# Prompt attention scores from a 64-row and a 128-row product in place of three 128-row products

## The chip, the cores and the metric

The kernel runs on one core of a Trainium2 chip. The metric is the device time of one execution in microseconds; a kernel's time is the median of its runs.

## The reference, cut to what matters

The reference is one inference step of a hybrid decoder layer: a prompt of 1024 tokens and a decode batch of 8 x 8 tokens go through a projection, dilated window attention (8 heads of 64), retention, an output projection and an MLP. The change touches the attention of the prompt alone. There, for each head, three branches (window, dilation) of the same queries, keys and values are combined by their softmax denominators:

```python
def _dilated_branch_prompt(q, k, v, window, dil):
    ...
    s = jnp.einsum('brcqhd,brckhd->brchqk', qb, kw).astype(F32) * (HEAD_DIM ** -0.5)
    ...
    valid = (dist[None] >= 0) & (dist[None] <= n) & (kg >= 0)
    p, lse = _masked_softmax(s, valid[None, None, :, None])
    o = jnp.einsum('brchqk,brckhd->brcqhd', p, vw.astype(F32))
```

## The kernel before, in words

The kernel runs its stages one after the other: modulation, projection, prompt attention, sample heads, sample (cache) attention, prompt retention, output projection, MLP. Each stage is a block with one instruction stream per engine, ordered by semaphores, and a barrier of all engines stands between stages (line 177 for those that clear their semaphores). The change lies in stage_prompt_attention, from line 692.

The stage computes the three branches at once: a score gets a bias, the logarithm of the number of branches in which its key is valid, or -1e30. Heads are handled in four pairs, as a loop of two rounds (i) with two pairs (s = 0, 1) written out in each. A pair's queries and keys lie as token tiles of 128 tokens x 128 columns, two heads of 64 side by side. PE transposes them (turn_heads, line 788, 8 transposes for queries into PSUM banks 0 and 1, 8 for keys into banks 2 and 3), so that rows 0 to 63 hold head 0 and rows 64 to 127 head 1.

Scores are made in the type fp32r from a high and a low part of each operand: high is the value rounded to fp32r, low is what is left. ScalarE takes the high parts out of PSUM (take_queries, line 829, which also scales and is done once for each head, 64 rows by 1024 columns; take_keys, line 835, all 128 rows at once). VectorE takes the low parts (low_parts, line 888: two passes of 64 rows for queries, one pass of 128 rows for keys, k_lo, line 896). Queries are held in tiles of 128 rows per head, whose other 64 rows are zero, so that a product over 128 rows with the keys of both heads gives the scores of one; the zeros are written once, by four memsets of VectorE at the stage's start (line 862), and ScalarE waits for them before it does anything (line 819).

A pair has 16 units (head, query tile of 128 rows). Head 0 goes through query tiles 0 to 7, head 1 through 7 to 0 (line 719). A unit with tile q has (q + 1) x 128 keys, in chunks of up to 512 keys, one PSUM bank each: tiles 0 to 3 have one chunk, tiles 4 to 7 two. For each chunk PE makes three products into the same bank (lines 770 and 771):

```python
for a, (x, y) in enumerate(((q_hi, k_hi), (q_hi, k_lo), (q_lo, k_hi))):
    mm = pe.matmul(out, x[h][:, q * P:(q + 1) * P], y[:, c:e], start=(a == 0), stop=(a == 2))
```

A unit then goes on: VectorE adds the bias and takes the row maximum (score, line 869, the instruction of line 874), ScalarE takes the exponential with its sum (line 827), VectorE divides (normalise, line 881), PE transposes the probabilities into banks 4 and 5 (turn, line 774), ScalarE copies them out (probT, line 849), PE multiplies with the values (values, line 780, products of 128 rows by 64 columns of weights into banks 6 and 7).

The order of PE's stream is written by hand: scores run three units ahead (scores(u + 3), turn(u + 1), values(u) in the loop from line 803). For s = 0 the transposes of the next pair's queries and keys stand near the end of the loop (line 806). ScalarE takes the next pair's queries after the probT copy of unit 14 and its keys after that of unit 15 (lines 850 to 853), and then copies the finished output of the pair out of PSUM (mix_hi, line 855). VectorE makes the next pair's low parts after its last normalise (line 905), then mix_lo, which waits for mix_hi (line 907), and then the first score of the next pair. Before the second round of the loop the order is another: mix_hi and mix_lo first, then the transposes, queries, keys and low parts. PE starts a pair's scores when all of its low parts are there (line 798). SP loads pairs ahead and GpSimd rotates their queries and keys; for pairs 2 and 3 SP waits for heads_free (line 733), which PE raises at a pair's end.

Of the kernel before, what the change touches and what calls it, by code (L numbers as in the profile page):

```python
# [20 lines left out]
F32 = mybir.dt.float32  # L21
F32R = mybir.dt.float32r
ALU = mybir.AluOpType
# [3 lines left out]
P = 128  # L27
D = 1024
KT = D // P
S = 1024  # L30
TT = S // P
# [4 lines left out]
H, HD = 8, 64  # L36
# [650 lines left out]
def banks(ps, first, n):  # L687

    return ps[:, first:first + n, :].rearrange("p b c -> p (b c)")


def stage_prompt_attention(nc, io, ps, ident, mix_hi, mix_lo, heads, smp):
# [6 lines left out]
    with st.ctx:  # L699
# [4 lines left out]
        q_hi = [st.sb(f"qhi{h}", [P, S], F32R) for h in range(2)]  # L704
        q_lo = [st.sb(f"qlo{h}", [P, S], F32R) for h in range(2)]
        k_hi, k_lo = st.sb("khi", [P, S], F32R), st.sb("klo", [P, S], F32R)
# [4 lines left out]
        zeroed, heads_free, turned, hi_done, split_done = (st.sem(n) for n in (  # L711
            "zeroed", "heads_free", "turned", "hi_done", "split_done"))
# [42 lines left out]
        def _(pe):  # L755
            pe.sem_inc(prob_turned, 3)
            pe.sem_inc(pv_done, 2)
            with pe.Fori(0, 2) as i:
                for s in range(2):
                    base = i * 2 * UNITS + s * UNITS  # L760

                    def scores(u):
                        h, q = unit(u)
                        if u >= 2:
                            pe.wait_ge(scored, base + u - 1)
                        width = (q + 1) * P
                        for c in range(0, width, CH):
                            e = min(width, c + CH)
                            out = banks(ps, 2 * (u % 2), 2)[:, c:e]
                            for a, (x, y) in enumerate(((q_hi, k_hi), (q_hi, k_lo), (q_lo, k_hi))):  # L770
                                mm = pe.matmul(out, x[h][:, q * P:(q + 1) * P], y[:, c:e], start=(a == 0), stop=(a == 2))
                        mm.then_inc(made, 1)
# [25 lines left out]
                    pe.wait_ge(split_done, 3 * (2 * i + s) + 3)  # L798
# [19 lines left out]
        def _(act):  # L818
            act.wait_ge(zeroed, 4)
            with act.Fori(0, 2) as i:  # L820
                for s in range(2):
# [7 lines left out]
                    def take_queries(s):  # L829
                        act.wait_ge(turned, 2 * (2 * i + s) + 1)  # L830
                        for h in range(2):
                            rows = slice(HD * h, HD * (h + 1))
                            act.mul(q_hi[h][rows, :], banks(ps, 0, 2)[rows, :], SCALE).then_inc(hi_done, 1)

                    def take_keys(s):
                        act.wait_ge(turned, 2 * (2 * i + s) + 2)
                        act.copy(k_hi[:], banks(ps, 2, 2)).then_inc(hi_done, 1)
# [20 lines left out]
        def _(dve):  # L858
            for x in (q_hi, q_lo):
                for h in range(2):  # L860
                    rows = slice(HD * (1 - h), HD * (2 - h))
                    dve.memset(x[h][rows, :].bitcast(F32), 0.0).then_inc(zeroed, 1)
            dve.wait_ge(zeroed, 4)
            dve.wait_ge(bias_in, 16)
            with dve.Fori(0, 2) as i:
                for s in range(2):
# [21 lines left out]
                    def low_parts(s):  # L888
                        for h in range(2):
                            rows = slice(HD * h, HD * (h + 1))  # L890
                            dve.wait_ge(hi_done, 3 * (2 * i + s) + h + 1)
                            dve.scalar_tensor_tensor(out=q_lo[h][rows, :], in0=banks(ps, 0, 2)[rows, :], scalar=SCALE,
                                                     in1=q_hi[h][rows, :].bitcast(F32), op0=ALU.mult,
                                                     op1=ALU.subtract).then_inc(split_done, 1)
                        dve.wait_ge(hi_done, 3 * (2 * i + s) + 3)
                        dve.tensor_tensor(k_lo[:], banks(ps, 2, 2), k_hi[:].bitcast(F32), ALU.subtract).then_inc(split_done, 1)
# [1850 lines left out]
```

## Time and profile before

| | |
|---|---|
| Median of 3 runs | 1938.46 us (1932.27 to 1939.40) |
| The profiled execution's own time | 1934.55 us |
| Its span, first to last instruction | 1932.6 us |
| Mean granted TensorE clock | 0.935 |
| Busy PE, weight loads, VectorE, ScalarE, GpSimd | 1699.1, 1371.6, 837.4, 550.3, 563.3 us |
| Prompt attention stage in the profile | about 421 to 631 us |

PE is TensorE's matmul side and PEld its weight loads, which can run under matmuls. The ends of matmuls are modelled in the profile, so the distance from one start to the next tells more than the length of one. The granted clock is 1.00 where TensorE ran at 2.4 GHz and 0.50 where it ran at 1.2 GHz.

### The profile page before, as it was taken

The page shows a single profiled execution, that of the slowest core. Times are in us where ns is not written, and L with a number is a line of the kernel's source. Part 1 is how long each engine was busy: PE and PEld are TensorE (multiplying, and loading weights), DVE is VectorE, ACT ScalarE, POOL GpSimd, SP SyncE. Part 2 cuts the span into 40 slices and gives each one's busy share as a digit, 9 for nine tenths or more (in the row PEclk, how much of TensorE's full clock was granted, in tenths as well). Part 3 has the DMA queues.
Part 4 walks back from the last instruction along what each step waited for, and adds up shares of the span by engine and source line. Part 5 has one row for each costly group of instructions (what it writes and reads, how often), then busy time and mean ns, then how long its engine had stood idle before and what let it go on. Part 6 is the DMA issues. An engine that isn't in the chain of part 4 may idle for free. (4 is left out here: it accounts for less than half of the span.)

```text
span 1932.6 us, 22382 instructions
## 1 busy us (share of the span) xinstructions
PE 1699.1 (88%) x8256; PEld 1371.6 (71%) x8256; DVE 837.4 (43%) x1556; ACT 550.3 (28%) x814; POOL 563.3 (29%) x272
## 2 busy tenths in 40 slices
PE   6599999979999478876699689999999999999983
PEld 1488888867777366655578568787878787878862
DVE  3921222026555345565556323333333333333489
ACT  0322222225555145552334321111111111111121
POOL 0332323335000015586000242222222222222354
PEclk9699999989999689996799899999999999999997
DMA  7534443362210667783052211111111111111122
GB/s 271 191 125 162 165 158 117 125 182 57 67 33 0 152 187 218 219 252 118 7 186 87 77 44 44 44 43 43 43 43 43 43 43 43 43 43 43 44 87 93
DMA packets 136813, 192.69 MB, mean 100 GB/s; under 512 B 10155, under 2 KB 84955, under 8 KB 136612
## 3 DMA queue, kind: packets, MB, share of 16 engines
q1 hardware_dynamic: 124630, 169.42, 27.8%
q10 hardware_dynamic: 12128, 22.55, 3.1%
q8 instruction: 32, 0.52, 0.1%
q14 instruction: 23, 0.19, 0.0%
HBM read 162.94 MB, written 29.00 MB: 99 GB/s over the span
## 5 line engine op out<-in xcount | busy, mean ns | idle before, releaser
L2286 POOL TENSOR_TENSOR mlp_w_lo<-w_room,mlp_w_hi 128x2048 fp32r<-128x2048 f32 x31 | 143.6, 4634 | 320.7 <-ACT mlp_w_hi L2282 320.6
L2587 PE MATMUL ps<-mix_hi,mlp_w_hi 128*128 128x512 f32 x512 | 204.7, 400 | 15.2 <-DVE mlp_w_lo L2286 9.7
L2485 DVE TENSOR_TENSOR x<-x,ps 128x512 f32<-128x512 f32 x224 | 153.9, 687 | 142.4 <-PE ps L2658 141.4
L2464 DVE TENSOR_TENSOR mlp_h_lo<-mlp_pos,mlp_h_hi 128x512 fp32r<-128x512 f32 x64 | 69.3, 1083 | 332.9 <-ACT mlp_h_hi L2388 330.8
L2587 PE MATMUL ps<-mix_lo,mlp_w_hi 128*128 128x512 f32 x512 | 204.6, 400 | 0.0
L2587 PE MATMUL ps<-mix_hi,mlp_w_lo 128*128 128x512 f32 x512 | 203.3, 397 | 0.0
L2658 PE MATMUL ps<-mlp_w_hi,mlp_h_hi 128*128 128x512 f32 x448 | 175.9, 393 | 5.5 <-DVE mlp_h_lo L2464 4.0
L2658 PE MATMUL ps<-mlp_w_hi,mlp_h_lo 128*128 128x512 f32 x448 | 174.4, 389 | 0.0
L2658 PE MATMUL ps<-mlp_w_lo,mlp_h_hi 128*128 128x512 f32 x448 | 174.4, 389 | 0.0
L603 POOL TENSOR_TENSOR inp_a_lo<-inp_room,inp_a_hi 128x2048 fp32r<-128x2048 f32 x24 | 110.5, 4604 | 216.3 <-ACT inp_a_hi L649 216.3
L628 PE MATMUL ps<-inp_whi,z_hi 128*128 128x512 f32 x384 | 151.5, 395 | 10.6 <-DVE inp_wlo L575 7.8
L628 PE MATMUL ps<-inp_wlo,z_hi 128*128 128x512 f32 x384 | 150.6, 392 | 0.0
L628 PE MATMUL ps<-inp_whi,z_lo 128*128 128x512 f32 x384 | 150.4, 392 | 0.0
L1828 POOL TENSOR_TENSOR cache_v_lo<-cache_V,cache_v_hi 128x2048 fp32r<-128x2048 f32 (+1 forms) x19 | 74.1, 3902 | 227.4 <-ACT cache_v_hi L1770 227.4
L2338 POOL TENSOR_TENSOR mlp_pos<-mlp_pos 128x512 f32<-128x512 f32 x64 | 66.6, 1040 | 215.5 <-ACT mlp_pos L2394 215.5
L2587 PEld LDWEIGHTS ps<-mix_hi,mlp_w_hi 128*128 128x128 f32 x512 | 97.1, 190 | 41.0 <-DVE mlp_w_lo L2286 10.1
L2394 ACT ACTIVATE mlp_pos<-ps 128x512 f32<-128x512 f32 x64 | 38.3, 598 | 295.9 <-PE ps L2587 295.9
L583 DVE TENSOR_TENSOR x_s<-ps,x_s 9x256 f32<-9x256 f32 x24 | 9.9, 412 | 242.3 <-ACT x_s L666 242.3
L2587 PEld LDWEIGHTS ps<-mix_hi,mlp_w_lo 128*128 128x128 f32 x512 | 97.0, 189 | 23.0
L2587 PEld LDWEIGHTS ps<-mix_lo,mlp_w_hi 128*128 128x128 f32 x512 | 97.1, 190 | 22.7
L2658 PEld LDWEIGHTS ps<-mlp_w_hi,mlp_h_hi 128*128 128x128 f32 x448 | 84.1, 188 | 25.3 <-issue 8.3
L2409 ACT CAST mlp_hs<-ps 128x128 fp32r<-128x128 f32 x16 | 4.2, 266 | 332.3 <-PE ps L2602 332.3
(365 smaller groups left out, 3506.1 us busy)
## 6 DMA issues: line engine op xcount, KB each, us to landing
w_room<-in_w_ff SPq DMA_DIRECT2D x32, 1024.0 KB, 6.8
inp_room<-in_w_ada SPq DMA_DIRECT2D x16, 1024.0 KB
proj<-inp_row ACTq DMA_DIRECT2D x54, 256.0 KB, 2.3
x<-in_cache_k SPq DMA_DIRECT2D x48, 256.0 KB, 5.3
cache_V<-in_cache_v SPq DMA_DIRECT2D x48, 256.0 KB, 4.7
mod_w<-in_w_ada SPq DMA_DIRECT2D x4, 2048.0 KB, 15.2
x<-in_x_prompt SPq DMA_DIRECT2D x16, 512.0 KB, 9.5
inp_room<-in_w_ada_f SPq DMA_DIRECT2D x8, 1024.0 KB
```

Of the source, the lines that this page charges most:

```text
L583: dve.tensor_tensor(a_row[j % 2], ps[0:NC, 6 + j % 2, 0:AW_CH], a_row[j % 2], ALU.add).then_inc(added, 1)
L603: pool.tensor_tensor(a_lo[:], a_raw[s], a_hi[:].bitcast(F32), ALU.subtract).then_inc(a_ready, 1)
L628: mm = pe.matmul(bank, z[:, k, cols], w[s][:, k, :], start=(k == 0 and a == 0), stop=(k == KT - 1 and a == len(parts) - 1))
L1828: eng.tensor_tensor(v_part(1, q, c), V[:, first:first + count, :], v_part(0, q, c).bitcast(F32), ALU.subtract).then_inc(v_ready, 1)
L2286: pool.tensor_tensor(lo, raw, hi.bitcast(F32), ALU.subtract).then_inc(ready, 1)
L2338: pool.tensor_tensor(x, x, x, ALU.mult).then_inc(sq_done, 1)
L2394: act.activation(pos[u % 2][:], ps[:, u, :], ACT.Relu).then_inc(relu_done, 1)
L2409: act.copy(hs[s][:, :, 0:NS], turned_s(ps)).then_inc(hs_hi, 1)
L2464: dve.tensor_tensor(h_lo[s][:, j, cols], pos[u % 2][:], h_hi[s][:, j, cols].bitcast(F32), ALU.subtract).then_inc(h_ready, 1)
L2485: dve.tensor_tensor(dst, dst, ps[:, 5 + o % 3, :], ALU.add).then_inc(added, 1)
L2587: mm = pe.matmul(ps[:, u, :], w[:, k, j * P:(j + 1) * P], z[:, k, rows], start=(k == 0 and a == 0), stop=(k == KT - 1 and a == 2))
L2658: mm = pe.matmul(out, h, w, start=(a == 0), stop=(a == len(parts) - 1))
```

## The change

The two mixed products, high queries with low keys and low queries with high keys, become one product over 128 rows. For it each head has a tile of queries (q_both) with the low part in its own 64 rows and the high part in the other head's rows, and a tile of keys (k_both) with the high part in its own rows and the low part in the other rows. The high parts are multiplied in a product over the head's own 64 rows. q_hi becomes one tile for both heads.

ScalarE takes the queries in one pass of 128 rows, the keys in two passes of 64 rows (one per head), and then copies the high queries of each head to the other partition half (two passes of 64 rows from SBUF to SBUF, semaphore moved). VectorE makes the low queries in two passes as before, both waiting for the one pass of ScalarE, and the low keys in two passes of 64 rows, which read one partition half and write the other. The four memsets and their wait are gone. PE waits for split_done (four passes) and for the first move before a pair's scores, and for the second move before unit 8.

```diff
--- before.py
+++ after.py
@@ -701,15 +701,17 @@
         bias_in, roped = heads.bias_in, heads.roped
         tmp = [st.sb(f"tmp{s}", [P, 2 * TT, 2, HALF]) for s in range(4)]
 
-        q_hi = [st.sb(f"qhi{h}", [P, S], F32R) for h in range(2)]
-        q_lo = [st.sb(f"qlo{h}", [P, S], F32R) for h in range(2)]
-        k_hi, k_lo = st.sb("khi", [P, S], F32R), st.sb("klo", [P, S], F32R)
+        q_hi = st.sb("qhi", [P, S], F32R)
+        q_both = [st.sb(f"qboth{h}", [P, S], F32R) for h in range(2)]
+        k_both = [st.sb(f"kboth{h}", [P, S], F32R) for h in range(2)]
+        OWN = [slice(HD * h, HD * (h + 1)) for h in range(2)]
+        OTHER = OWN[::-1]
         prob = [st.sb(f"prob{s}", [P, S]) for s in range(3)]
         probT = [st.sb(f"probT{s}", [P, S]) for s in range(2)]
         top, neg, total, inv = (st.sb(n, [P, UNITS]) for n in ("top", "neg", "total", "inv"))
         waited = st.sb("waited", [P, 1])
-        zeroed, heads_free, turned, hi_done, split_done = (st.sem(n) for n in (
-            "zeroed", "heads_free", "turned", "hi_done", "split_done"))
+        heads_free, turned, hi_done, split_done, moved = (st.sem(n) for n in (
+            "heads_free", "turned", "hi_done", "split_done", "moved"))
         made, scored, neg_done, exp_done, inv_done, prob_done, prob_turned, probT_done, pv_done, mix_hi_done = (
             st.sem(n) for n in ("made", "scored", "neg_done", "exp_done", "inv_done", "prob_done",
                                 "prob_turned", "probT_done", "pv_done", "mix_hi_done"))
@@ -763,12 +765,15 @@
                         h, q = unit(u)
                         if u >= 2:
                             pe.wait_ge(scored, base + u - 1)
+                        if u == TT:
+                            pe.wait_ge(moved, 2 * (2 * i + s) + 2)
                         width = (q + 1) * P
                         for c in range(0, width, CH):
                             e = min(width, c + CH)
                             out = banks(ps, 2 * (u % 2), 2)[:, c:e]
-                            for a, (x, y) in enumerate(((q_hi, k_hi), (q_hi, k_lo), (q_lo, k_hi))):
-                                mm = pe.matmul(out, x[h][:, q * P:(q + 1) * P], y[:, c:e], start=(a == 0), stop=(a == 2))
+                            at = slice(q * P, (q + 1) * P)
+                            pe.matmul(out, q_hi[OWN[h], at], k_both[h][OWN[h], c:e], start=True, stop=False)
+                            mm = pe.matmul(out, q_both[h][:, at], k_both[h][:, c:e], start=False, stop=True)
                         mm.then_inc(made, 1)
 
                     def turn(u):
@@ -795,7 +800,8 @@
                     if s == 0:
                         turn_heads(0, 0)
                         turn_heads(0, 1)
-                    pe.wait_ge(split_done, 3 * (2 * i + s) + 3)
+                    pe.wait_ge(split_done, 4 * (2 * i + s) + 4)
+                    pe.wait_ge(moved, 2 * (2 * i + s) + 1)
                     scores(0)
                     scores(1)
                     scores(2)
@@ -816,7 +822,6 @@
 
         @block.scalar
         def _(act):
-            act.wait_ge(zeroed, 4)
             with act.Fori(0, 2) as i:
                 for s in range(2):
                     base = i * 2 * UNITS + s * UNITS
@@ -828,13 +833,15 @@
 
                     def take_queries(s):
                         act.wait_ge(turned, 2 * (2 * i + s) + 1)
-                        for h in range(2):
-                            rows = slice(HD * h, HD * (h + 1))
-                            act.mul(q_hi[h][rows, :], banks(ps, 0, 2)[rows, :], SCALE).then_inc(hi_done, 1)
+                        act.mul(q_hi[:], banks(ps, 0, 2), SCALE).then_inc(hi_done, 1)
 
                     def take_keys(s):
                         act.wait_ge(turned, 2 * (2 * i + s) + 2)
-                        act.copy(k_hi[:], banks(ps, 2, 2)).then_inc(hi_done, 1)
+                        for h in range(2):
+                            act.copy(k_both[h][OWN[h], :], banks(ps, 2, 2)[OWN[h], :]).then_inc(hi_done, 1)
+                        act.wait_ge(hi_done, 3 * (2 * i + s) + 1)
+                        for h in range(2):
+                            act.copy(q_both[h][OTHER[h], :], q_hi[OWN[h], :].bitcast(F32)).then_inc(moved, 1)
 
                     if s == 0:
                         take_queries(0)
@@ -856,11 +863,6 @@
 
         @block.vector
         def _(dve):
-            for x in (q_hi, q_lo):
-                for h in range(2):
-                    rows = slice(HD * (1 - h), HD * (2 - h))
-                    dve.memset(x[h][rows, :].bitcast(F32), 0.0).then_inc(zeroed, 1)
-            dve.wait_ge(zeroed, 4)
             dve.wait_ge(bias_in, 16)
             with dve.Fori(0, 2) as i:
                 for s in range(2):
@@ -886,14 +888,15 @@
                                           ALU.mult).then_inc(prob_done, 1)
 
                     def low_parts(s):
+                        dve.wait_ge(hi_done, 3 * (2 * i + s) + 1)
                         for h in range(2):
-                            rows = slice(HD * h, HD * (h + 1))
-                            dve.wait_ge(hi_done, 3 * (2 * i + s) + h + 1)
-                            dve.scalar_tensor_tensor(out=q_lo[h][rows, :], in0=banks(ps, 0, 2)[rows, :], scalar=SCALE,
-                                                     in1=q_hi[h][rows, :].bitcast(F32), op0=ALU.mult,
+                            dve.scalar_tensor_tensor(out=q_both[h][OWN[h], :], in0=banks(ps, 0, 2)[OWN[h], :], scalar=SCALE,
+                                                     in1=q_hi[OWN[h], :].bitcast(F32), op0=ALU.mult,
                                                      op1=ALU.subtract).then_inc(split_done, 1)
-                        dve.wait_ge(hi_done, 3 * (2 * i + s) + 3)
-                        dve.tensor_tensor(k_lo[:], banks(ps, 2, 2), k_hi[:].bitcast(F32), ALU.subtract).then_inc(split_done, 1)
+                        for h in range(2):
+                            dve.wait_ge(hi_done, 3 * (2 * i + s) + h + 2)
+                            dve.tensor_tensor(k_both[h][OTHER[h], :], banks(ps, 2, 2)[OWN[h], :], k_both[h][OWN[h], :].bitcast(F32),
+                                              ALU.subtract).then_inc(split_done, 1)
 
                     if s == 0:
                         low_parts(0)
```

## Rows read from the trace of the kernel before

**Rows 1.** Stretch: length, busy PE, PEld, DVE, ACT, POOL; clock, DMA, GB/s.

```profile
488.00:526.00 38.00, 38.00 (x266) 31.75 (x265) 20.50 (x75) 20.05 (x40) 3.80 (x5) 1.00 0.10 29
```

**Rows 2.** Waits of 421 to 631 us: us in total, times, longest.

```profile
PE ps L771 <- DVE att_klo L896: 15.8, 4, 7.2
```

**Rows 3.** Timeline, PE, score products (start, length in us), one unit each.

```profile
449.95 0.50 PE L771 MATMUL ps<-att_khi,att_qhi 128*128 128x512 f32 x1
450.29 0.39 PE L771 MATMUL ps<-att_klo,att_qhi 128*128 128x512 f32 x1
450.52 0.40 PE L771 MATMUL ps<-att_khi,att_qlo 128*128 128x512 f32 x1
...
458.65 0.28 PE L771 MATMUL ps<-att_klo,att_qhi 128*128 128x256 f32 x1
458.77 0.28 PE L771 MATMUL ps<-att_khi,att_qlo 128*128 128x256 f32 x1
...
473.96 0.28 PE L771 MATMUL ps<-att_klo,att_qhi 128*128 128x128 f32 x1
474.07 0.28 PE L771 MATMUL ps<-att_khi,att_qlo 128*128 128x128 f32 x1
```

**Rows 4.** Timeline, PE, retention stage, 64-row and 128-row products.

```profile
922.91 0.49 PE L1280 MATMUL ps<-ret_state,ret_qdT 64*128 64x128 f32 x2
923.33 0.49 PE L1278 MATMUL ps<-x,ret_sT 128*128 128x128 f32 x2
...
928.13 1.84 PE L1265 MATMUL ps<-ret_qT,ret_kT 64*128 64x128 f32 x15
```

**Rows 5.** Timeline, PE, sample attention, 8-row products behind 128-row ones.

```profile
736.71 0.40 PE L1664 MATMUL ps<-cache_v_lo,cache_probT 128*128 128x512 f32 x1
737.04 0.49 PE L1668 MATMUL ps<-cache_vn_hi,cache_probT 8*128 8x512 f32 x1
737.38 0.39 PE L1668 MATMUL ps<-cache_vn_lo,cache_probT 8*128 8x512 f32 x1
```

**Rows 6.** Timeline, start of the stage.

```profile
421.08 3.67 PE L792 MATMUL ps<-ident,x 128*128 128x128 f32 x16 [3.76 <-PEq L486]
...
425.77 1.28 ACT L833 ACT_TABLE_LOAD   x1 [7.83 <-DVE att_qlo L862]
...
431.90 0.47 PE L771 MATMUL ps<-att_khi,att_qhi 128*128 128x128 f32 x1 [7.15 <-DVE att_klo L896]
```

**Rows 7.** Timeline, end of pair 0 and start of pair 1.

```profile
478.32 2.48 DVE L892 SCALAR_TENSOR_TENSOR att_qlo<-ps,att_qhi 64x1024 fp32r<-64x1024 f32 x2 [2.19 <-ACT att_qhi L833]
...
479.35 0.27 ACT L849 COPY att_probT<-ps 128x128 f32<-128x128 f32 x1
...
480.42 1.03 ACT L855 CAST mix_hi<-ps 128x1024 f32 x1
...
481.96 1.21 DVE L908 TENSOR_TENSOR mix_lo<-ps,mix_hi 128x1024 f32 x1
...
482.10 0.33 PE L771 MATMUL ps<-att_khi,att_qhi 128*128 128x128 f32 x1 [2.00 <-DVE att_klo L896]
...
483.10 0.28 DVE L874 CUSTOM_DVE_ANT_0 att_prob<-ps,x 128x128 f32<-128x128 f32 x1
```

**Rows 8.** Groups by line and shape, ScalarE, a copy from SBUF to SBUF.

```profile
L2073 ACT CAST outp_whi<-w_room 128x1024 fp32r<-128x1024 f32 x8 | 8.1, 1046 | 9.8 <-DMA w_room<-in_w_out 8.2 <-PEq L1031 1.6
```

**Rows 9.** Timeline, first score product of pair 2.

```profile
534.02 0.47 PE L771 MATMUL ps<-att_khi,att_qhi 128*128 128x128 f32 x1 [4.63 <-DVE att_klo L896]
```

**Rows 10.** The stretches' view again: two boundaries, then retention.

```profile
476.90:488.00 11.10, 8.01 (x40) 5.54 (x40) 8.64 (x26) 7.30 (x15) 0.74 (x2) 0.85 0.47 142
577.60:590.40 12.80, 10.30 (x47) 7.26 (x46) 8.63 (x26) 7.65 (x16) 0.00 (x0) 0.73 0.00 0
...
901.00:916.70 15.70, 10.48 (x30) 7.41 (x30) 7.13 (x4) 1.71 (x2) 3.18 (x1) 0.50 0.22 71
...
921.50:928.10 6.60, 6.60 (x38) 4.86 (x38) 3.95 (x9) 2.26 (x7) 0.00 (x0) 1.00 0.04 11
```

## The prediction

> **What bounds the kernel now.** I read the page first (TensorE is busy 88% of the span), then the stretches of the one stage that the diff touches, then its waits, then single instructions. The attention stage lasts from 421 to 631 us, four head pairs of 16 units each. In the steady part of a pair TensorE has no gap at all: 38.00 us busy of 38.00 in pair 1, while VectorE has 20 and ScalarE 20 [rows 1]. So there a TensorE instruction more or less moves the end one for one. Between pairs it is not TensorE: it stands still 15.8 us in four waits, all for the low part of the keys on VectorE [rows 2]. Two prices decide, then: what a product costs on TensorE, and what the split of queries and keys costs on ScalarE and VectorE between pairs. The stage ends at a barrier of all engines and nothing after it is under way before, so I take its change to the end of the kernel one for one.
>
> **Products removed.** Today a unit makes three products per chunk of up to 512 keys; there are 96 chunks (48 of 512 keys, 16 each of 384, 256 and 128). From start to start a product of 512 takes 0.23 us, of 256 0.12, of 128 0.11 [rows 3]; 384 I put between, 0.175. One product per chunk goes: 48 x 0.23 + 16 x (0.175 + 0.12 + 0.11) = 17.5 us. That the remaining one has 64 rows saves nothing: products of 64 rows ran at 0.112 us each for 128 columns (15 in 1.84 us, the last one's 0.27 us tail taken off) [rows 4], as the 128-row ones did [rows 3].
>
> **Switches added.** The new pair alternates 64 rows and 128 rows. The retention stage does the same today: a 128-row product, then a 64-row product into the same accumulation, with no wait between. Each product there is two instructions, which at 0.112 would take 0.22 us; they take 0.42 [rows 4], so 0.20 us goes at each change of row count. The other place is an 8-row product behind 128-row ones, 512 columns, the same type as the scores: 0.33 us up to it and 0.34 behind its start, 0.67 where 0.46 is the steady pace [rows 5], so 0.21 for one change. Both sit close, in both directions; I take 0.20. A unit's scores are entered from the 64-column value products, a change that exists already (the first product starts 0.34 before the second, where 0.23 is the pace [rows 3]). So a unit with one chunk gains one switch; a unit with two chunks gains three. A pair has 8 of each, so 8 + 24 = 32 switches, 128 in all: 25.6 us. TensorE's net work is 25.6 - 17.5 = +8.1 us. Of that the first three units of a pair lie under VectorE's latency (they have one chunk, 128 to 384 keys: 3 x 0.20 - 0.405 = 0.2 us per pair, 0.8 in all): **+7.3 us**. Bounds: without a cost of switching -17.5, with 0.22 each 28.2 - 17.5 = +10.7. The page "TensorEngine Tiling (Array Packing)" of the Trainium skill, Key Properties, says that changing the tiling mode drains the engine, which speaks against this change, and gives no price; the trace agrees with 0.20 us.
>
> **Start of the stage.** Four memsets and the wait on them go. Today the queries are taken only behind them: the table load starts at 425.77, scores at 431.90 [rows 6]. Without them the load (1.28 us) runs under the transposes that began at 421.08 at half clock, half of whose 3.67 us make the queries ready near 423.1. One ScalarE pass (1.03 us for 1024 columns [rows 7]; VectorE's take 1.24 with 64 rows and 1.21 with 128, so the rows don't count [rows 7]) and then VectorE's four passes of 1.24 (two for queries, now two for keys where there was one): 423.1 + 1.03 + 4 x 1.24 = 429.1. ScalarE's two key passes and two moves end about then and hold up nothing. **-2.8 us**. Bounds: -4 (if the transposes are taken earlier) and -1.2 (no overlap of the table load).
>
> **Between pairs 0 and 1, 2 and 3.** Here ScalarE's order matters. Today: queries, last probT copy (479.35), keys, mix_hi (480.42), and VectorE: low parts, mix_lo at 481.96, first score at 483.10 [rows 7]. The new order has one query pass, so the copy waits only for its transpose (about 479.0), then two key passes, two moves, and only then mix_hi. A move is a ScalarE copy from SBUF to SBUF into the other partition half; no such copy to other partitions stands in the trace, and the nearest is a copy of 1024 columns within its partitions, 1.05 us [rows 8]. I take 1.05, with nothing and twice as much as bounds, for lack of a nearer row. So 479.15 + 2 x 1.02 + 2 x 1.05 = 483.2, mix_hi until 484.2, and **behind mix_hi waits mix_lo on VectorE, and behind mix_lo the first score**, which comes at 484.3 + 1.14 = 485.4 instead of 483.1: +2.3 us each, **+4.5 us** for two. TensorE's own start of scores moves only 1.2 us (VectorE's fourth pass), which the late score covers. If moves cost nothing, the boundary is set by that fourth pass and costs 1.2 each, 2.4 in all; if twice as much, 8.7.
>
> **Between pairs 1 and 2.** Queries and keys are taken after mix_lo here, so only VectorE's extra pass counts, scores start 1.2 us behind 534.02 [rows 9]; moves end before. **+1.2 us**.
>
> **Clock.** TensorE stands still longer at the two boundaries. The stretch around the first had granted clock 0.85, around the second 0.73 [rows 10]. A pair's first units then run at the lower pace; what part of that VectorE's latency hides I can't read, so I add **+1.0 us** for a longer time at 1.2 GHz (0 to 3).
>
> GpSimd has no instruction in the diff; SP's loads of the next pair wait on heads_free, two pairs ahead of use, so both queues only shift.
>
> **Sum**: +7.3 - 2.8 + 4.5 + 1.2 + 1.0 = +11.2 us. The profiled execution took 1934.55 us, so 1945.8 against it. The median of the runs is 1938.46, 3.9 above that execution; carried onto it, the changed kernel comes at **1949.7 us**. Half a per cent (9.7 us) is about what a measurement of this kernel tells from no change; the sum sits just beyond it.
>
> **Rivals.**
> *The switch is free for these products* (chance 0.07). TensorE does 17.5 us less, of which 1.6 in the first three units is hidden: -15.9, with the +3.9 of start, boundaries and clock: -12.0, **1926.5 us**. For it: the loads of 128-row weights hide entirely at the pace of [rows 3]. Against it stand [rows 4, 5]. The page "TensorE: Matmul & The Clock Gate" of the Trainium skill, Part 2, has a rule that would do this: weight loads are pulled ahead of running matmuls if they go to the background buffer; by that rule 1926.5 us, but [rows 4] don't show it.
> *Half a switch* (0.08): only the drain or only the exposed load, 0.10 us. 12.8 - 17.5 + 3.9 = -0.8, **1937.7 us**, no change to see.
> *The clock falls* (0.13). The engine streams for a smaller part of each unit. In the retention stage the same alternation ran at granted clock 0.50 for all of 906 to 917, and at 1.00 in 922 to 928 [rows 10], so it neither raises the clock by itself nor drops it at once. If each pair spends some 7 us more at half clock at its start, TensorE would lose 3.5 us if it alone set the time, and as VectorE sets a good part of these units, some 2; that is +8 on the sum: **1958 us**. It decides once a pair's start stays at 1.2 GHz for ten us.
> *The boundaries cost nothing*, because the late score is absorbed by later slack or the moves run under something (0.05): 7.3 - 2.8 + 1.2 = +5.7, **1944 us**.
> The forecast has 0.67: its own range, from the bounds of moves, start, clock and a switch of 0.17 to 0.22 us, is +6 to +15. About two thirds of that lies over 9.7.
>
> **Chances.** Slower by over 0.5%: 0.44 of the forecast plus the clock, 0.57. Within 0.5%: 0.23 of the forecast, half a switch and idle boundaries, 0.36. Faster: 0.07. The range must reach from just above half a switch to the clock case, 1940 to 1959; it leaves out the free switch, most of the half switch and the tails.
>
> **What would show it.** The 64-row and 128-row score products should start about 0.43 us apart at 512 columns; 0.23 makes the free switch right. PE busy should still fill the steady stretch. ScalarE should show four passes of 1.0 between the last probT copy and mix_hi, and the first score of pairs 1 and 3 should come about 1.2 us after mix_hi ends. The first score product should start near 429. Were TensorE idle in the steady part, or the clock under 0.9 there, the sum would be wrong in kind.

## The result and the profile after

The changed kernel takes 1968.88 us (median of 4 runs, 1961.43 to 1971.02) against 1938.13 us before: 1.6% slower, ratio 1.0159, 95% interval 1.0134 to 1.0185, or +30.8 us. The forecast said slower, by 11.2 us, and the time lies outside its range. The profiled execution is the fastest of the four, 1961.43 us. In it the attention stage ends 35.5 us later than before (its last mix_hi starts at 663.85 instead of 628.36), and some 8 us of that come back in later stages; the other three executions are 7 to 10 us slower as a whole, so the median need not hold that.

The page, its first lines and the row of the granted clock:

```profile
span 1959.8 us, 22209 instructions
...
PE 1729.4 (88%) x8160; PEld 1370.8 (70%) x8160; DVE 836.4 (43%) x1556; ACT 558.7 (29%) x822; POOL 563.6 (29%) x272
...
PEclk9799999978877878997879899999999999999997
```

There are 96 instructions fewer on PE and 30 us more of PE busy. The clock row is the first clue: in slices 9 to 14, where most of the attention stage lies, it reads 7 or 8, where before it reads 9, and 8 once.

The view by stretch shows why. Its columns are as in [rows 1]: length, busy PE, PEld, DVE, ACT and POOL, granted clock, DMA. The stretches are all those of the changed kernel's attention stage at granted clock 0.50, and one at 1.00 (the third) between them:

```profile
419.60:450.30 30.70, 24.73 (x73) 15.82 (x73) 16.04 (x44) 14.14 (x25) 11.18 (x10) 0.50 0.75 195
487.80:508.30 20.50, 19.62 (x53) 11.67 (x54) 11.06 (x41) 7.76 (x19) 4.23 (x6) 0.50 0.31 92
508.30:541.00 32.70, 32.70 (x213) 24.62 (x211) 15.09 (x56) 15.81 (x31) 0.00 (x0) 1.00 0.01 2
545.90:569.80 23.90, 20.11 (x55) 12.20 (x55) 12.73 (x43) 10.27 (x22) 4.17 (x6) 0.50 0.21 64
607.30:634.60 27.30, 26.32 (x73) 16.20 (x74) 12.75 (x48) 10.58 (x23) 0.00 (x0) 0.50 0.00 0
```

And the same view of the kernel before, again all stretches of the stage at 0.50:

```profile
419.70:436.80 17.10, 8.43 (x32) 6.66 (x32) 10.38 (x25) 6.32 (x11) 3.64 (x6) 0.50 0.98 247
484.60:488.00 3.40, 3.26 (x9) 2.14 (x10) 2.56 (x13) 2.12 (x7) 0.74 (x2) 0.50 0.58 173
532.40:539.20 6.80, 4.74 (x15) 3.35 (x15) 5.03 (x20) 1.97 (x7) 4.19 (x6) 0.50 0.11 32
583.60:590.40 6.80, 6.50 (x20) 4.32 (x20) 4.16 (x23) 3.25 (x10) 0.00 (x0) 0.50 0.00 0
```

102.4 us at 1.2 GHz after, 34.1 us before. Every pair now has 20 to 30 us at half clock at its start, and there TensorE hardly stands still once its products run (19.62 us busy of 20.50 in pair 1). Once a pair is at 2.4 GHz it stays there to its end, although the alternation goes on.

The timeline of PE gives the two prices of a switch, which is a change between 64 and 128 rows from one product to the next. At 2.4 GHz, answering to [rows 3]:

```profile
453.42 0.50 PE L775 MATMUL ps<-att_kboth,att_qhi 64*128 64x512 f32 x1
453.85 0.50 PE L776 MATMUL ps<-att_kboth,att_qboth 128*128 128x512 f32 x1
454.28 0.49 PE L775 MATMUL ps<-att_kboth,att_qhi 64*128 64x512 f32 x1
454.70 0.50 PE L776 MATMUL ps<-att_kboth,att_qboth 128*128 128x512 f32 x1
```

and at 1.2 GHz:

```profile
498.52 0.79 PE L775 MATMUL ps<-att_kboth,att_qhi 64*128 64x512 f32 x1
499.25 0.80 PE L776 MATMUL ps<-att_kboth,att_qboth 128*128 128x512 f32 x1
499.97 0.58 PE L775 MATMUL ps<-att_kboth,att_qhi 64*128 64x256 f32 x1
```

0.43 us from start to start at full clock is 0.20 more than the 0.23 of [rows 3]. At half clock it is 0.72 to 0.73, where two products of 128 rows stood 0.43 us apart in the kernel before:

```profile
586.19 0.63 PE L771 MATMUL ps<-att_klo,att_qhi 128*128 128x512 f32 x1
586.62 0.63 PE L771 MATMUL ps<-att_khi,att_qlo 128*128 128x512 f32 x1
```

The weight loads show what changes. Behind a switch a load starts together with its own product (453.85 and 454.28 above):

```profile
453.85 0.19 PEld L776 LDWEIGHTS ps<-att_kboth,att_qboth 128*128 128x128 f32 x1 [0.25 <-issue]
454.28 0.18 PEld L775 LDWEIGHTS ps<-att_kboth,att_qhi 64*128 64x128 f32 x1 [0.24 <-issue]
```

In the kernel before, the load for the product at 450.52 [rows 3] starts 0.22 us ahead of it, under the product before:

```profile
450.30 0.19 PEld L771 LDWEIGHTS ps<-att_khi,att_qlo 128*128 128x128 f32 x1
```

Where in a pair the time goes can be read from VectorE's score passes. In pair 1, those of units 9 and 15, before and then after:

```profile
504.12 1.08 DVE L874 CUSTOM_DVE_ANT_0 att_prob<-ps,x 128x896 f32<-128x896 f32 x1 [1.37 <-issue]
523.20 0.29 DVE L874 CUSTOM_DVE_ANT_0 att_prob<-ps,x 128x128 f32<-128x128 f32 x1 [1.01 <-issue]
517.93 1.08 DVE L876 CUSTOM_DVE_ANT_0 att_prob<-ps,x 128x896 f32<-128x896 f32 x1 [1.55 <-issue]
537.52 0.29 DVE L876 CUSTOM_DVE_ANT_0 att_prob<-ps,x 128x128 f32<-128x128 f32 x1 [1.04 <-issue]
```

19.08 us before and 19.59 after, at 2.4 GHz and alike in all four pairs: half a microsecond more. From unit 0 to unit 9, where the half clock lies, the four pairs together take 86.3 us before and 116.2 after. So 30 of the stage's 35.5 us arise in the first nine units of the pairs, in the profiled executions.

Between pairs 0 and 1 the timeline of all engines, answering to [rows 7]:

```profile
483.18 0.27 ACT L856 COPY att_probT<-ps 128x128 f32<-128x128 f32 x1 [0.63 <-PE ps L782]
483.34 2.04 ACT L841 CAST att_kboth<-ps 64x1024 fp32r<-64x1024 f32 x2
...
485.28 2.11 ACT L844 CAST att_qboth<-att_qhi 64x1024 fp32r<-64x1024 f32 x2
487.42 1.01 ACT L862 CAST mix_hi<-ps 128x1024 f32 x1
487.69 0.36 PE L775 MATMUL ps<-att_kboth,att_qhi 64*128 64x128 f32 x1 [3.75 <-DVE att_kboth L898]
...
488.60 1.23 DVE L911 TENSOR_TENSOR mix_lo<-ps,mix_hi 128x1024 f32 x1 [1.04 <-ACT mix_hi L862]
...
489.75 0.29 DVE L876 CUSTOM_DVE_ANT_0 att_prob<-ps,x 128x128 f32<-128x128 f32 x1
```

Four ScalarE passes stand between the last probT copy and mix_hi, mix_lo waits for mix_hi (1.04 us idle ahead of it), and the first score for mix_lo. That score comes 6.57 us behind the last probT copy, 2.8 more than the 3.75 of [rows 7]. TensorE stands still for 3.75 us, 1.75 more than in [rows 7], until VectorE's fourth pass is done. A move to the other partition half takes 1.05 us, like a copy within the partitions [rows 8].

### The profile page after: what moved, and what is told of

It is laid out like the page before. It is cut to its first block and busy times, and to the rows that moved or that the text cites. A ratio compares the mean times of both kernels' runs of the same rounds, so it can differ in the third digit from the quotient of the medians.

```text
span 1959.8 us, 22209 instructions
## 1 busy us (share of the span) xinstructions
PE 1729.4 (88%) x8160; PEld 1370.8 (70%) x8160; DVE 836.4 (43%) x1556; ACT 558.7 (29%) x822; POOL 563.6 (29%) x272
```

## The experiments

All medians are set against the kernel before on the same chip; microseconds are the ratio less one, times 1936. "Half clock" is the time at granted clock 0.50 in the profiled execution, summed over the whole stretches that overlap the stage; the kernel before has 34. "The stage" in us is the time from its first transpose to its last mix_hi in that one execution: 207.3 before, 242.8 in the changed kernel.

| run | products and their rows | ratio (interval) | us | half clock |
|---|---|---|---|---|
| changed kernel | 64, 128 | 1.0159 (1.0134 to 1.0185) | +30.8 | 102 |
| e1_switch_in_before | 64, 128, 128, staging as before | 1.0245 (1.0215 to 1.0274) | +47 | 89 |
| e2_no_switch | 128, 128 | 0.9933 (0.9912 to 0.9954) | -13 | 51 |
| e3_grouped | a unit's 64s, then its 128s | 1.0045 (1.0026 to 1.0065) | +9 | 85 |
| e4_64_twice | 64, 64, 128 | 1.0314 (1.0292 to 1.0337) | +61 | 123 |
| e5_fill | 64, 128, fill before a pair | 1.0193 (1.0151 to 1.0235) | +37 | 96 |
| e6_reorder | 128, 128, mix_hi first | 0.9945 (0.9927 to 0.9964) | -11 | 48 |
| e7_reorder_fill | the same with the fill | 0.9932 (0.9911 to 0.9952) | -13 | 34 |
| e8_staging_only | 128, 128, 128 | 1.0015 (0.9996 to 1.0034) | +3 | 41 |
| e9_second_head | 64 rows in units 8 to 15 | 1.0014 (0.9996 to 1.0032) | +3 | 51 |
| e10_first_head | 64 rows in units 0 to 7 | 1.0157 (1.0113 to 1.0201) | +30 | 106 |
| e11_fill_more | 64, 128, more fill | 1.0070 (1.0046 to 1.0093) | +14 | 14 |
| e12_best | 128, 128, mix_hi first, more fill | 0.9901 (0.9879 to 0.9922) | -19 | 17 |

**e1_switch_in_before: the alternation alone.**

```diff
-                                mm = pe.matmul(out, x[h][:, q * P:(q + 1) * P], y[:, c:e], start=(a == 0), stop=(a == 2))
+                                rows = slice(HD * h, HD * (h + 1)) if a == 0 else slice(0, P)
+                                mm = pe.matmul(out, x[h][rows, q * P:(q + 1) * P], y[rows, c:e], start=(a == 0), stop=(a == 2))
```

> The kernel before with one edit: the first of the three products reads only the head's own 64 rows. Staging of queries and keys stays as before; the alternation of 64 and 128 rows comes in alone, 128 added switches, no product gone. Theory A (the alternation keeps TensorE at 1.2 GHz): 128 x 0.20 = 25.6 us of switches, and beside them the attention stage shows 70 us or more at granted clock 0.50 where before shows 34, worth 10 us or more: +36 to +45 us. Theory B (the longer standstill between pairs, by the new staging, lowers the clock; the alternation costs its switches alone): about +25 us, with half clock near the 34 us of before. Theory C (a switch costs more than 0.20 us at 512 columns): score products more than 0.45 us apart at full clock.

+47 us, with 88.8 us at half clock. One slice of rows in one product, nothing else, costs 47 us, where its switches at full clock are 25.6 us at the forecast's price. From unit 9 to 15, at 2.4 GHz, this kernel takes 20.92 us where the one before takes 19.08: 1.84 us for ten switches, 0.18 each. All 128 would be 23.6 us. That is theory A, and a little beyond its range. Staging and standstill were those of before (TensorE waits 2.00 us ahead of pair 1's scores in both), so theory B falls as the main cause. Score products of 512 columns stand 0.42 us apart at full clock, so theory C falls too.

**e2_no_switch: the change without the alternation.** The high product reads all 128 rows of a zero-padded tile; ScalarE fills it in two passes.

```diff
-                            pe.matmul(out, q_hi[OWN[h], at], k_both[h][OWN[h], c:e], start=True, stop=False)
+                            pe.matmul(out, q_hi[h][:, at], k_both[h][:, c:e], start=True, stop=False)
```

> The changed kernel, but the high product runs over 128 rows: queries of each head in a tile of their own whose other 64 rows are zero, times the keys tile of both parts. No switch; one product per chunk less than before; the staging between pairs as changed (a second ScalarE pass for queries more, two memsets at the start). Theory A: -16 us on TensorE, +5 to +7 of staging, half clock near that of before: -9 to -12 us against before. Theory B: the half clock of the changed kernel (102 us in the stage) stays for the most part, +15 us: 0 to +7 us against before.

-13 us, a little beyond theory A's -9 to -12: the change's idea, two products for three, is sound. What makes it slower is that the first of them has 64 rows. A stretch of this run, the start of pair 1, by the same columns:

```profile
478.10:488.30 10.20, 7.82 (x24) 4.95 (x24) 6.90 (x30) 5.32 (x14) 4.30 (x6) 0.50 0.44 132
```

The half clock is 10.2 us here, against 20.5 in the changed kernel and 3.4 before. The alternation makes most of the difference. The rest is shared: e8_staging_only, further down, has the same standstill with three products per chunk and shows 6.8 us in this place and 41 in the stage, against 51 here and 34 before. So in these executions some 7 us of half clock go with the new staging and some 10 with the missing product.

**e3_grouped: half of the switches.**

```diff
-                        for c in range(0, width, CH):
...
+                        for c, e, out in chunks:
+                            pe.matmul(out, q_hi[OWN[h], at], k_both[h][OWN[h], c:e], start=True, stop=False)
+                        for c, e, out in chunks:
+                            mm = pe.matmul(out, q_both[h][:, at], k_both[h][:, c:e], start=False, stop=True)
```

> The changed kernel with the order inside a unit changed: first the 64-row products of all its chunks, then the 128-row ones. Units of two chunks have one added switch in place of three: 64 switches in all where the changed kernel has 128. Theory A: 12.8 us of switches less than the changed kernel and a part of the half clock gone with them, so 16 to 25 us below the changed kernel, +6 to +15 us against before. Theory B: 12.8 us less than the changed kernel and the same half clock, about +18 us against before.

+9 us, 22 below the changed kernel, inside A's figure and outside B's. 12.8 us of it are 64 switches less at the full-clock price; the rest goes with 17 us less of half clock. How it divides was not measured.

**e4_64_twice: more streaming between two switches.**

```diff
+                            pe.matmul(out, q_hi[OWN[h], at], k_both[h][OWN[h], c:e], start=True, stop=True)
                             pe.matmul(out, q_hi[OWN[h], at], k_both[h][OWN[h], c:e], start=True, stop=False)
```

> The changed kernel with each 64-row product made twice in a row (the second overwrites the first), so no switch is added but TensorE streams more between two switches: 96 more products, 17.5 us at full clock. Theory A: the half clock in the stage shrinks from 102 us, to 60 or less if streaming is what it wants, which gives back 8 us or more: at most +10 us against the changed kernel. Theory B: the half clock stays at about 102 us and the time rises by 17 to 20 us.

A miss for both: 30 us above the changed kernel, with more half clock (123 us), not less. The longest stretch of it, in pair 2:

```profile
556.00:597.00 41.00, 38.55 (x112) 24.44 (x112) 15.78 (x54) 13.00 (x27) 4.16 (x6) 0.50 0.09 27
```

More 64-row work between the switches did not bring the clock up. So it is open whether it is the switches or the 64-row products that keep the clock down; "alternation" stands for both here. The same added product over 128 rows in this place, which would tell them apart, was not run.

**e5_fill: work in the standstill.** Transposes of the identity go into an unused part of PSUM ahead of the wait for a pair's scores.

```diff
+                    for n in range((22, 30)[s]):
+                        pe.transpose(banks(ps, 4, 2)[:, CH:CH + P], ident[:], ident[:])
                     pe.wait_ge(split_done, 4 * (2 * i + s) + 4)
```

> The changed kernel, with idle transposes of the identity into an unused part of PSUM in TensorE's standstill before each pair's scores (22 before pairs 0 and 2, 30 before pairs 1 and 3; 2.4 to 4.8 us, inside the standstill). Is it the standstill that puts the clock down, with the alternation only keeping it there? Theory A1 (yes): pairs 1 to 3 begin at 2.4 GHz and stay there, the half clock in the stage falls from 102 us to 50 or less, and the time falls by 12 us or more below the changed kernel: +19 us or less against before. Theory A2 (the alternation in a pair's first units brings the clock down by itself): half clock 80 us or more, within 5 us of the changed kernel.

No gain (7 us above the changed kernel, with an interval that is 16 us wide), 96 us of half clock: A1 falls, and the number is near A2's. Pair 1's start in the timeline of PE shows more than that:

```profile
483.24 3.47 PE L804 MATMUL ps<-ident 128*128 128x128 f32 x30
486.84 0.32 PE L775 MATMUL ps<-att_kboth,att_qhi 64*128 64x128 f32 x1
...
487.66 0.38 PE L776 MATMUL ps<-att_kboth,att_qboth 128*128 128x256 f32 x1
489.25 0.61 PE L775 MATMUL ps<-att_kboth,att_qhi 64*128 64x384 f32 x1 [1.20 <-DVE att_top L878]
489.78 0.69 PE L776 MATMUL ps<-att_kboth,att_qboth 128*128 128x384 f32 x1
```

and the stretches around it:

```profile
483.20:489.40 6.20, 4.82 (x35) 4.15 (x35) 5.05 (x8) 4.31 (x5) 0.00 (x0) 1.00 0.84 252
489.40:513.30 23.90, 23.42 (x66) 14.06 (x67) 11.57 (x42) 8.48 (x21) 4.23 (x6) 0.50 0.15 45
```

The pair began at 2.4 GHz. The clock fell at 489.4, after 1.20 us of waiting for VectorE's first score, and stayed down for 23.9 us in which TensorE did not wait. Two suspects were left for the fall: the alternation of the first units, or their waits.

**e11_fill_more: work in those waits too.**

```diff
+                    for n in range((4, 12)[s]):
+                        pe.transpose(banks(ps, 4, 2)[:, CH:CH + P], ident[:], ident[:])
                     scores(2)
+                    for n in range(6):
+                        pe.transpose(banks(ps, 4, 2)[:, CH:CH + P], ident[:], ident[:])
                     turn(0)
```

> e5_fill with idle transposes also where TensorE waits for VectorE in the first units of a pair (4 or 12 before the third unit's scores, 6 before the first turn). If the waits of the first units are what puts the clock down in e5_fill, and alternation at 2.4 GHz does not: pairs 1 to 3 stay at 2.4 GHz, half clock in the stage under 50 us, 10 us or more below the changed kernel. If the alternation of the first units puts it down by itself: half clock 80 us or more and no gain.

17 us below the changed kernel, by nothing but idle transposes. In the stretches' view, pair 1 and then pair 2:

```profile
482.00:529.00 47.00, 45.93 (x281) 33.29 (x280) 26.10 (x97) 24.02 (x50) 4.35 (x6) 1.00 0.13 39
535.60:542.40 6.80, 5.43 (x18) 3.92 (x18) 3.83 (x17) 1.25 (x5) 4.17 (x6) 0.50 0.15 46
542.40:588.00 45.60, 45.45 (x290) 33.93 (x290) 24.82 (x83) 25.37 (x48) 0.00 (x0) 1.00 0.05 16
```

Pair 1 runs at 2.4 GHz from end to end with every switch in it, and so do the products of pairs 0 and 3. So alternation does not bring the clock down; the waits at a pair's start do. Pair 2 bounds the other half of the reading. Its products began at half clock, and the clock came back 5.4 us later while they alternated, with ten idle transposes over 128 rows among them:

```profile
536.97 0.47 PE L775 MATMUL ps<-att_kboth,att_qhi 64*128 64x128 f32 x1 [3.42 <-DVE att_kboth L904]
...
538.65 1.05 PE L810 MATMUL ps<-ident 128*128 128x128 f32 x4
...
540.74 1.48 PE L813 MATMUL ps<-ident 128*128 128x128 f32 x6
```

So alternation delays the return of the clock but does not rule it out: 20 us and more without such transposes, 6.8 with them, and 3 to 10 in the stretches of pairs 1 to 3 before and in e2. (This profiled execution, 1934.06 us, is the fastest of nine, which go to 1950.47. By their mean clocks, 0.932 to 0.937 against 0.940, the others had 13 to 33 us more at 1.2 GHz in the whole kernel, an estimate; in which stage is not on record.)

**e9_second_head and e10_first_head: where the alternation stands.** e2_no_switch with 64 rows for one head of each pair; for the second:

```diff
-                            pe.matmul(out, q_hi[h][:, at], k_both[h][:, c:e], start=True, stop=False)
+                            rows = OWN[h] if h == 1 else slice(0, P)
+                            pe.matmul(out, q_hi[h][rows, at], k_both[h][rows, c:e], start=True, stop=False)
```

> The kernel of e2_no_switch with 64-row high products for the second head of each pair alone (units 8 to 15, when a pair has long been at 2.4 GHz). 64 switches, half of the changed kernel's, all late. If alternation at 2.4 GHz costs its switches and no more: 64 x 0.20 = 12.8 us above e2_no_switch, near +1 us against before, with half clock in the stage at 45 to 60 us as there. If alternation brings the clock down wherever it runs: 80 us or more at half clock, +20 us or more above e2_no_switch.

> The same with 64-row products for the first head alone (units 0 to 7, from a pair's start). The same 64 switches, all early. If it is the alternation at a pair's start that holds the clock at 1.2 GHz: half clock near 100 us as in the changed kernel, and 25 to 32 us above e2_no_switch (12 of switches and most of the 19 us of clock). If place does not matter: the same time as e9_second_head.

The same 64 switches cost 16 us late in a pair and 43 us at its start. The late ones leave the half clock as it was (51 us in both); the early ones take it to 106. Pair 1's start with the early ones:

```profile
486.30:510.20 23.90, 21.12 (x56) 12.49 (x56) 12.49 (x42) 10.16 (x22) 4.23 (x6) 0.50 0.35 106
```

and with the late ones:

```profile
483.40:493.60 10.20, 7.50 (x22) 4.71 (x23) 7.18 (x29) 4.77 (x14) 4.36 (x6) 0.50 0.48 144
```

The 43 us lie above the expectation and leave nothing for the late switches of the changed kernel, which has both kinds at the same total; the interval of e10 is 17 us wide, and the profiled stages don't show that equality: 202.3 us in e2, 213.6 with the late switches (+11.3), 236.3 with the early ones (+34.0), 242.8 in the changed kernel. I take the direction as shown and not the exact split.

**e8_staging_only: the staging's price.** e2_no_switch with its first product made twice.

```diff
+                            pe.matmul(out, q_hi[h][:, at], k_both[h][:, c:e], start=True, stop=True)
                             pe.matmul(out, q_hi[h][:, at], k_both[h][:, c:e], start=True, stop=False)
```

> e2_no_switch with the first 128-row product of each chunk made twice (the second overwrites the first): three products of 128 rows per chunk as before, and the new staging of queries and keys. It prices the staging alone: +5 to +9 us against before by the sum of the prediction without switches (two times 2.3 at the boundaries inside a round, 1.2 at the other, about 1 for the clock). Against e2_no_switch it prices one product per chunk: 16 to 19 us.

+3 us, not resolved from zero, and below what the expectation gave, which had left out the gain at the stage's start. That gain is 1.0 us here (first score product 9.79 us behind the first transpose, 10.82 before), for this kernel still has two memsets and a second pass for the queries. The profiled stage is 6.1 us longer than before, so the price of the staging lies somewhere from 3 to 6 us. One product per chunk, e8 against e2, is worth 0.0082 x 1936 = 16 us.

**e6_reorder: mix_hi ahead of the moves.**

```diff
+                    if s == 0:
+                        move(1)
```

(behind the mix_hi copy, with the two moves taken out of take_keys).

> The kernel of e2_no_switch (two products of 128 rows) with one edit: at the boundary inside a round ScalarE takes mix_hi before the two moves instead of behind them. If mix_hi behind the moves is what delays the first score there, that score comes about 1.3 us earlier in pairs 1 and 3: 2 to 4 us below e2_no_switch. If the wait is for the fourth VectorE pass, no difference.

In the trace the first score of pair 1 comes 5.1 us behind the last probT copy instead of 6.6:

```profile
474.39 0.27 ACT L861 COPY att_probT<-ps 128x128 f32<-128x128 f32 x1
...
476.61 1.01 ACT L867 CAST mix_hi<-ps 128x1024 f32 x1
477.65 2.11 ACT L848 CAST att_qboth<-att_qhi 64x1024 fp32r<-64x1024 f32 x2
478.37 1.23 DVE L921 TENSOR_TENSOR mix_lo<-ps,mix_hi 128x1024 f32 x1
...
479.52 0.29 DVE L886 CUSTOM_DVE_ANT_0 att_prob<-ps,x 128x128 f32<-128x128 f32 x1
```

Twice 1.4 us is too little for the medians: 2 us above e2_no_switch, with intervals that overlap. The profiled stage is 3.9 us shorter (198.4 against 202.3), in one execution of each. The mechanism is seen, its price is not.

**e7_reorder_fill: the fill without alternation.** e6_reorder with the edit of e5_fill.

> e6_reorder with the idle transposes of e5_fill. If the standstill alone sets the half clock of a pair's start in a kernel without alternation, the half clock in the stage falls from about 51 to 30 us or less and the time by 3 to 7 us below e6_reorder. If VectorE's latency hides that clock, no difference over 2 us.

The half clock falls to 34 us (32 if counted from the stage's first transpose) and the time by some 2 us: no difference that counts. But set beside e5_fill this run is the test of the mechanism without alternation. Pair 1 begins at 2.4 GHz here too, TensorE waits 0.39, 0.67 and 0.46 us among the first units, and the clock falls at 483.0:

```profile
483.00:489.80 6.80, 6.73 (x23) 4.82 (x23) 3.62 (x13) 2.62 (x8) 4.16 (x6) 0.50 0.27 80
```

It is back after 6.8 us, with 128-row products alone, where e5_fill needed 23.9. The waits of the two runs are alike but not the same. So the fall needs no alternation; the late return comes with it, or with its 64-row products (see e4).

**e12_best: all that helped.** e7_reorder_fill with the idle transposes of e11_fill_more (6 in place of 12).

> e7_reorder_fill (two 128-row products, mix_hi before the moves, idle transposes before each pair's scores) with the idle transposes of e11_fill_more in the first units too (4 or 6, then 6). Is there more to be had from the clock without alternation? The half clock in the stage should fall from 32 us to 15 or less. If those microseconds cost time, 2 to 5 us below e7_reorder_fill, so 14 to 18 us below the kernel before; if VectorE's latency hides them in a pair's first units, or the idle transposes are in the way, within 2 us of it.

1918.11 us, -19 us against before, faster than both kernels. It is 6 us below e7, but with intervals that overlap, and its half clock is 17 us, a little over the 15 expected. What its idle transposes make is never read.

## Why the prediction was wrong

By its steps:

- **The bound.** Right. TensorE has no gap in the steady part (32.70 busy of 32.70), and its long waits are the four on the keys' low parts at the pairs' starts.
- **Products removed.** -17.5 us, some 16 of it on the path. Right: 16 us by the medians (e8 against e2); between units 9 and 15, 1.34 us of a pair (19.08 less 17.74), where the forecast's prices make 1.3.
- **Switches added.** 0.20 us each at 2.4 GHz, from the retention stage [rows 4] and the 8-row product [rows 5]. Right, and a little high: at 512 columns 0.43 us from start to start where 0.23 is the pace, but over all widths 0.18 (units 9 to 15 at 2.4 GHz: 19.58 us in the changed kernel, 17.74 in e2, ten switches apart, and the same 1.84 us in e1). That makes 23.6 us for 128 and not 25.6. Late switches cost 16 us for 64 by the medians and 11 by the profiled stages, where 12.8 was their sum. The page "TensorEngine Tiling (Array Packing)" of the Trainium skill, Key Properties, says that a change of the tiling mode drains the engine; the trace agrees in that every change cost time. The free switch of the first rival did not occur.
- **Start, boundaries.** Right in mechanism, and a little small: scores at 429.24 (429.1 was the sum), four ScalarE passes, first score 1.3 us behind the end of mix_hi. Against the last probT copy the first score came 2.8 us later in pairs 1 and 3 (2.3 was the sum) and 1.4 in pair 2 (1.2). As measured, -2.6 + 5.6 + 1.4 = +4.4 us; the forecast had -2.8 + 4.5 + 1.2 = +2.9.
- **Clock.** This term failed: "I add **+1.0 us** for a longer time at 1.2 GHz (0 to 3)". The measured one is near 20 us: 30.8 less 6.1 for TensorE (23.6 - 17.5) and 4.4 for start and boundaries. It holds all that costs more at 1.2 GHz, the dearer switches too, and whatever the sum lacks. Nearly all of it lies in the pairs' first nine units: 86.3 us before, 116.2 in the changed kernel, 88.4 in e11. (In the profiled execution it is more: of the 29.9 us there, switches and products at full clock make some 4.) e11_fill_more supports its size by another way: the changed kernel with nearly all of its clock back is 17 us faster and comes to +14 us, 3 above the forecast.

The prediction had seen the mechanism and filed it as a rival with 0.13 of the chance and +8 us. The rows against its small size lay in its own table: in 906 to 917 the alternation ran at granted clock 0.50 for its whole length, in 922 to 928 at 1.00 [rows 10]. I read them as "neither raises nor drops it at once" and took that as comfort. Read as two separate statements they are close to the result: alternation at 2.4 GHz kept the clock, alternation at 1.2 GHz did not get it back in those 10.5 us, and takes 20 and more in the changed kernel. The second was the one to price, because every pair of the kernel before has a stretch at 1.2 GHz at its start (three of 3.4 to 6.8 us and one of 17.1 in the rows above). The price to put on it was a pair's whole first part at half clock, four times, and not 1 us.

What the time at 1.2 GHz costs per microsecond depends on what else bounds it: about 20 us for 68 us more here, less than half a microsecond for each. VectorE's latency covers a part of the first units, and a switch at half clock costs 0.29 us (0.72 less 0.43) and not twice the 0.20. How much each of the two saves was not measured. In e1, with three products per chunk, it is 24 us for 55 (47.4 less 23.6).

## What to carry to other kernels

Count the changes of row count in TensorE's stream before trading a 128-row product for a 64-row one: with zero-padded rows the same product is cheaper here by 44 us in all. When products are spaced out, ask not only what the spaces cost but at which clock each stretch starts, and how long a stretch like it in the trace took to come back to 2.4 GHz. Idle transposes in the waits around a pair's first units (32 to 48 per pair) bought 17 us in the kernel that alternates; in the one that doesn't, the last 10 or 12 of them per pair brought 6 us that are not resolved.

## What the runs showed of the hardware

- The same 64 switches cost 16 us where they stand late in a pair and 43 where they stand early (11 and 34 by the profiled stages); the early ones come with 55 us more at 1.2 GHz.
- Behind a switch the weight load starts with its own product (453.85); between products of 128 rows it starts 0.22 us ahead, and the product comes 0.20 us sooner.
- Over ten switches between products of 128 to 512 columns at 2.4 GHz, a switch cost 0.18 us, with two products per chunk (19.58 us against 17.74) as with three (20.92 against 19.08).
- A pair that had been kept at 2.4 GHz through its boundary (e5_fill) lost it at 489.4, behind a wait of 1.20 us in its first alternating units, and needed 23.9 us to regain it; with that wait filled (e11_fill_more) it never lost it. Without alternation (e7_reorder_fill) it lost it too, and had it back in 6.8 us.
- Doubling the 64-row products lengthened the time at 1.2 GHz from 102 to 123 us.
- ScalarE and VectorE move 64 x 1024 elements to the other half of the partitions at the price of a pass within them: 1.05 us (2.11 for two) and 1.24 us (2.48 for two).
